# Two neighbouring tiles of the experts' tables loaded by one transfer

## The chip, the cores and the metric

The kernel runs on one core of one Trainium2 chip. The metric is the device time of one execution in microseconds; a kernel's time is the median of several runs. Besides the timed runs there is one profiled execution, which the hardware profiler recorded; all rows below are from it.

## The reference, cut to what matters

The block takes x, 512 tokens of 1024 numbers, through attention and then through a PEER layer, which holds most of the work. All is float32.

```
mix = concat(fox_attention, swa_sink_attention) @ w_out     # 512 x 1024
x   = layer_norm(ALPHA * x + mix)
# PEER: 8 heads, each picks 16 of 16384 experts per token
q   = x @ w_q ;  s1, s2 = scores of q against keys1, keys2 (128 each per head)
eidx, gate = the 16 best sums of s1 and s2, and their softmax
a   = u_tab[eidx] . x          # one number per token, head and choice
w   = gelu(a) * gate
y   = sum of w * v_tab[eidx]   # 512 x 1024
x   = layer_norm(ALPHA * x + y)
```

`u_tab` and `v_tab` have 16384 rows of 1024 floats, 64 MB each.

## The kernel before, in words

The first 350 us hold the attention and the routing (queries, scores, top 16). They load weights tile by tile as the rest does and are not touched by the change.

For 384 of the 512 tokens the kernel does not gather rows: it multiplies these tokens with the whole of both tables. Each table is 128 tiles of 128 experts x 1024 numbers, 512 KB a tile. For the 128 tokens of the first block (and for 16 of the last ones in the first table) the rows of the chosen experts are gathered by indirect transfers of 512 KB (128 rows of 4 KB) that GpSimd issues, and VectorE works on them.

The tiles are numbered through the whole kernel. In this text **feature tile n** (n = 0 to 127) is tile `S_U + n`, of the first table, and **value tile n** is tile `S_V + n`, of the second. Both `S_U` (42) and `S_V` (170) are even, and a tile's place in the ring is its number modulo 4.

What happens to every table tile c:

1. SyncE (SP) issues its load into `raw[:, c % 4, :]`, a ring of four places (`load_tile`, L436 to L439). Before it, SP waits until the tile four before it, which had the place, has been split (`lo_ready`). The load adds 16 to a semaphore of its place when it has landed.
2. ScalarE (ACT) waits for the landing and for PE to have finished tile c - 4, and rounds the tile to its upper part `hi` (`split_hi`, L451). There are four places for the parts.
3. GpSimd (POOL) writes the lower part, `lo = raw - hi` (`split_lo`, L457), and thereby frees the place in `raw`. Between two such tiles it issues the gathers (L765).
4. TensorE (PE) multiplies with both parts, in three products, so that the result has nearly float32 precision. A feature tile is 24 matmuls at lines L1831 to L1833, a value tile 18 at L1886 to L1888.

Each engine works through one list of instructions in order. What stands behind the load's consumer on ACT matters for the change:

- Feature tile n: ACT does the GELU of tile n - 4 (`gelu_tile`, L1026), then rounds tile n (L451), then, in the middle of the table, copies finished gate sums out of PSUM (`stage_gates`, L1072), then the GELU of tile n - 3. PE may begin tile n + 2 once the GELU of tile n is done, and the next group of gate matmuls (L2104, L2105) once the copy of the group before it is done.
- The last 12 feature tiles (116 to 127) keep their GELUs in SBUF (`kept`). While they are multiplied, the loads of the first value tiles are issued.
- Value tile n: ACT rounds the weights of tile n - 2 (`weight_hi`, L1118), then the table tile n (L451), then the weights of tile n - 1, and so on. VectorE (DVE) makes the weights (L1694), their lower part after ACT's part (L1703), and between them adds a gathered row (L1735). PE begins a value tile when its weights' lower part and its table parts are there.

All loads of SP go through one hardware queue (q1) and are served in the order of issue; the gathers are on another (q0), the stores of GELUs on a third (q10); all share 16 DMA engines. In the middle of the features (tiles 44 to 115) SP also stores 2 MB of gates (L602) after every sixth tile. In the values the order on SP is, per eight tiles (`load_octet`): a wait for the weights and a 768 KB load `ga`, tiles 0 to 3, a wait and the next `ga`, tiles 4 and 5, a 1.5 MB load `gg8` of gates (L649), tiles 6 and 7. Ahead of the first value tiles stand two loads of gates of 768 KB (L622), behind value tile 7 the 1 MB of layer norm parameters (L639) and one more 768 KB.

Of the kernel before, what the change touches and what calls it, by code (L numbers as in the profile page):

```python
# [27 lines left out]
P = 128  # L28
SEQ = 512
D = 1024  # L30
KT = D // P
# [9 lines left out]
ETILES = 128  # L41
# [5 lines left out]
RAW_SLOTS = 4  # L47
# [5 lines left out]
S_U = S_PQ + LISTS  # L53
S_V = S_U + ETILES
# [29 lines left out]
A_PRE = 44  # L84
# [3 lines left out]
A_MID = MID_TILES * O_MID  # L88
# [30 lines left out]
def build(nc, x_t, x_rows, w1, w_ff, b_f, sinks, ln_par, w_pq, keys_t, u_t, u_rows, v_tab, consts, out):  # L119
# [5 lines left out]
    with ctx:  # L125
        def sb(name, shape, dt=F32, stack=ctx):
            return stack.enter_context(nc.sbuf_tensor(name, shape, dt))

        def sem(name):
            return ctx.enter_context(nc.semaphore(name))  # L130
# [9 lines left out]
        raw = sb("raw", [P, RAW_SLOTS, D])  # L140
# [149 lines left out]


        raw_loaded = [sem(f"raw_loaded{i}") for i in range(RAW_SLOTS)]
        hi_ready = sem("hi_ready")
        lo_ready = sem("lo_ready")
        tile_used = sem("tile_used")
# [95 lines left out]
        def wait(eng, s, value):  # L391

            if not (isinstance(value, int) and value <= 0):
                eng.wait_ge(s, value)
# [26 lines left out]
        def parts_of(c):  # L421
            if S_WOUT + PART_SLOTS <= c < S_PQ:
                return resident[c - S_WOUT]
            if c == N_TILES - 1:
                return last_parts
            if c >= S_U:
                return hi[c % EXPERT_SLOTS], lo[c % EXPERT_SLOTS]
            return hi[c % PART_SLOTS], lo[c % PART_SLOTS]
# [7 lines left out]
        def load_tile(eng, c, it, src):  # L436

            wait(eng, lo_ready, 4 * it + (c - RAW_SLOTS + 1))
            eng.dma_start(raw[:, c % RAW_SLOTS, :], src).then_inc(raw_loaded[c % RAW_SLOTS], 16)  # L439

        def split_hi(act, c, it):

            if isinstance(it, int):
                c, it = c + 4 * it, 0
            wait(act, raw_loaded[c % RAW_SLOTS], 16 * it + 16 * (c // RAW_SLOTS + 1))
            if S_PQ <= c < S_PQ + PART_SLOTS:

                act.wait_ge(tile_used, S_WOUT + (c - S_PQ) + 1)
            elif c != N_TILES - 1 and not S_WOUT + PART_SLOTS <= c < S_PQ:
                wait(act, tile_used, 4 * it + (c - (EXPERT_SLOTS if c >= S_U else PART_SLOTS) + 1))  # L450
            act.activation(parts_of(c)[0][:, :], raw[:, c % RAW_SLOTS, :], ACT.Copy).then_inc(hi_ready, 1)  # L451
# [17 lines left out]
        KEPT = A_POST // 4  # L469
        KEPT_FROM = ETILES // 4 - KEPT  # L470
# [54 lines left out]
        def _(sp):  # L525
# [36 lines left out]
                for k in range(4):  # L562
                    load_tile(sp, S_PQ + k, i, w_pq[4 * i + k])

            for k in range(8):
                load_tile(sp, S_U + k, 0, u_t[k])

            def load_features(k, it):

                load_tile(sp, S_U + 8 + k, it, u_t[4 * it + (8 + k)])  # L570

            def move_numbers():

# [19 lines left out]
            def two_chunks(o, first=False):  # L593
                for t in range(MID_TILES):
                    load_features(t % 4, 3 * o + (A_PRE // 4 + t // 4))
                    if first and t == 3:
                        move_gates()
                    if t % (MID_TILES // 2) == MID_TILES // 2 - 1:
                        half = t // (MID_TILES // 2)

                        sp.wait_ge(staged, 4 * GROUPS_PER_CHUNK * o + 2 * GROUPS_PER_CHUNK * (half + 1))
                        sp.dma_start(g_dram[2 * o + half], stage[half][:, :, :]).then_inc(g_stored[half], 16)  # L602

            with sp.Fori(0, A_PRE // 4 - 1) as it:
                for k in range(4):
                    load_features(k, it)
            for k in range(2):
                load_features(k, A_PRE // 4 - 1)
# [9 lines left out]
            def load_group(g, slot):  # L618

                if not (isinstance(g, int) and g >= KEPT_FROM):  # L620
                    sp.dma_start(ga[slot][:, :, :], a_dram[g]).then_inc(comb_loaded[slot], 16)
                sp.dma_start(gg[slot][:, :, :, :],  # L622
                             g_dram[:, :, bass.ds(4 * g, 4), :].rearrange("c p n t -> p c n t")
                             ).then_inc(comb_loaded[slot], 16)


            for k in range(A_PRE + A_MID + 8, ETILES):
                load_tile(sp, S_U + k, 0, u_t[k])


            for slot in range(GELU_SLOTS):
# [2 lines left out]
                sp.wait_ge(g_stored[half], 16 * CHUNKS // 2)  # L634
            load_group(KEPT_FROM, 0)
            load_group(KEPT_FROM + 1, 1)
            for k in range(8):
                load_tile(sp, S_V + k, 0, v_tab[4 * KEPT_FROM + k])
            sp.dma_start(ln2_gb[:, :, :], ln_par[:, 2:4, :]).then_inc(ln_loaded, 16)  # L639
            for slot, g in enumerate((KEPT_FROM + 2, 0)):  # L640

                sp.wait_ge(wgt_ready, 4 * slot + 4)
                load_group(g, slot)
                for k in range(4):
                    load_tile(sp, S_V + 8 + 4 * slot + k, 0, v_tab[4 * g + k])

            def load_gates(i, par):

                sp.dma_start(gg8[par][:, :, :, :],  # L649
                             g_dram[:, :, bass.ds(8 * i - 4 * KEPT, 8), :].rearrange("c p n t -> p c n t")  # L650
                             ).then_inc(gg8_loaded[par], 16)
# [4 lines left out]
            def load_octet(i, par, last=False):  # L656
                for slot in range(2):
                    sp.wait_ge(wgt_ready, 8 * i + (4 * slot - 4))
                    sp.dma_start(ga[slot][:, :, :], a_dram[2 * i + (slot - KEPT)]).then_inc(comb_loaded[slot], 16)
                    for k in range(4):  # L660
                        load_tile(sp, S_V + 4 * slot + k, 2 * i, v_tab[8 * i + (4 * (slot - KEPT) + k)])
                        if slot == 1 and k == 1 and not last:
                            load_gates(i + 1, 1 - par)

            with sp.Fori(1, ETILES // 16 - 1) as j:
                for par in range(2):
                    load_octet(2 * j + par, par)
            load_octet(ETILES // 8 - 2, 0)
            load_octet(ETILES // 8 - 1, 1, last=True)
            def store_halves(b, before):  # L670
                for h in range(2):
# [142 lines left out]
        def _(act):  # L814
            for i in range(X_CHUNKS):

                act.wait_ge(xT_loaded[i], 16)
                act.activation(xT_hi[:, x_chunk(i), :], xT[:, x_chunk(i), :], ACT.Copy).then_inc(xT_hi_ready, 1)
                if i == 0:
                    split_hi(act, 0, 0)  # L820
            for c in range(1, S_LOOP):
                split_hi(act, c, 0)
# [46 lines left out]

            split_heads(1, 0, swa_k_hi, twice=swa_k_hi)  # L870
            split_hi(act, S_LOOP, 0)
            copy_proj(2, vT[:, :], 1)
            split_hi(act, S_LOOP + 1, 0)
# [1368 lines left out]
```

## Time and profile before

| | us |
|---|---|
| median of 3 runs | 1445.74 (1444.88 to 1448.5) |
| the profiled execution, its whole time | 1447.31 |
| its span in the trace | 1445.6 |
| TensorE busy (granted clock 0.998) | 1424.1 |
| GpSimd busy | 1011.6 |
| VectorE busy | 1051.2 |
| ScalarE busy | 607.4 |

The span is the time from the first to the last recorded instruction; the whole time has a little around it (1.7 us here). Busy time of TensorE leaves 21.5 us of the span. Of these 12.5 us lie in the first 350 us, where the attention starts and the phases change, and some 7 us in the last 20 us, where the last norm runs. In a row of the timeline the first number is the start, the second the duration; what stands in brackets is the idle time of the engine before the row and what ended it. In a row of the stretches stand, after the stretch and its length, the busy time (and instructions) of PE, PE's weight loads, DVE, ACT and POOL, then PE's granted clock, the share of the DMA engines and GB/s.

### The profile page before, as it was taken

Reading aid. Unit: us, or ns where it says so; the run is one execution under the profiler, and the core shown is the slowest. Engines: PE = TensorE matmul, PEld = TensorE weight load, DVE = VectorE, ACT = ScalarE, POOL = GpSimd, SP = SyncE. Lnnn points to the kernel's source line nnn. Section 1 sums busy time; section 2 is a strip of 40 time slices with the busy share of each in tenths; the row PEclk is TensorE's granted clock in tenths of the full one; section 3 lists DMA queues with packets and bytes.
Section 4 is the critical chain, followed back from the end, with each engine's and each line's share of the span. In section 5 each row is a group of like instructions: output and inputs, shape, how many; then the busy total and the mean of one; then the engine's idle time right before and its main releaser. Section 6 shows DMA issues by size and latency. Waiting matters only on the chain.

```text
span 1445.6 us, 24823 instructions
## 1 busy us (share of the span) xinstructions
PE 1424.1 (99%) x8029; PEld 1266.3 (88%) x8029; DVE 1051.2 (73%) x2206; ACT 607.4 (42%) x1018; POOL 1011.6 (70%) x629
## 2 busy tenths in 40 slices
PE   9999999999999999999999999999999999999997
PEld 5888778889999999999999999878888888888885
DVE  5466666688999999899986694867555555555587
ACT  5666741334333354444444443333333333333333
POOL 3432331335598878887887689889888888888885
PEclk9999999999999999999999999999999999999999
DMA  6212120423599979999999899999999999999981
GB/s 241 74 59 103 59 89 4 144 86 126 171 351 320 298 265 378 393 420 405 391 364 386 321 397 387 344 371 368 355 362 359 356 356 343 351 356 339 359 336 71
DMA packets 136909, 406.97 MB, mean 282 GB/s; under 512 B 13905, under 2 KB 56657, under 8 KB 134673
## 3 DMA queue, kind: packets, MB, share of 16 engines
q1 hardware_dynamic: 80384, 240.67, 46.6%
q0 software_dynamic: 39760, 142.76, 25.1%
q10 hardware_dynamic: 16704, 22.81, 4.3%
q8 instruction: 29, 0.48, 0.1%
q14 instruction: 32, 0.25, 0.0%
HBM read 355.50 MB, written 50.14 MB: 281 GB/s over the span
## 4 chain that ended last, share of the span: by engine, by line
PE 82%; DVE 5%; POOL 4%; issue 4%; DMA 2%; ACT 2%; SPq 0%; ACTq 0%; POOLq 0%; DVEq 0%
PE banks L1831 13%; PE banks L1833 13%; PE banks L1832 13%; PE banks L1886 12%; PE banks L1888 11%; PE banks L1887 11%; POOL lo L457 3%; PE banks L1948 2%; POOL rows L765 2%; PE banks L2104 1%; PE banks L2105 1%; DMA raw<-v_tab 1%; PE banks L2041 1%; PE banks L1932 1%; DVE rows L1365 1%
## 5 line engine op out<-in xcount | busy, mean ns | idle before, releaser
L457 POOL TENSOR_TENSOR lo<-raw,hi 128x1024 fp32r<-128x1024 f32 x290 | 700.5, 2417 | 344.0 <-ACT hi L451 328.0
L1831 PE MATMUL banks<-x1T_hi,hi 128*128 128x368 f32 (+3 forms) x1168 | 395.3, 338 | 0.3 <-DVE x1T_lo L1337 0.3
L1832 PE MATMUL banks<-x1T_lo,hi 128*128 128x368 f32 (+3 forms) x1168 | 390.0, 334 | 0.0
L1833 PE MATMUL banks<-x1T_hi,lo 128*128 128x368 f32 (+3 forms) x1168 | 389.9, 334 | 0.0
L451 ACT ACTIVATE hi<-raw 128x1024 fp32r<-128x1024 f32 x291 | 305.8, 1051 | 22.4 <-DMA raw<-v_tab 13.0
L1886 PE MATMUL banks<-hi,wgt_hi 128*128 128x512 f32 x750 | 292.0, 389 | 1.7 <-DVE wgt_lo L1703 1.7
L1887 PE MATMUL banks<-lo,wgt_hi 128*128 128x512 f32 x750 | 291.8, 389 | 0.0
L1888 PE MATMUL banks<-hi,wgt_lo 128*128 128x512 f32 x750 | 291.8, 389 | 0.0
L1703 DVE TENSOR_TENSOR wgt_lo<-wgt,wgt_hi 128x384 fp32r<-128x384 f32 x125 | 101.0, 809 | 185.8 <-ACT wgt_hi L1118 185.5
L1831 PEld LDWEIGHTS banks<-x1T_hi,hi 128*128 128x128 f32 x1168 | 219.3, 188 | 4.8 <-DVE x1T_lo L1337 0.6
L1833 PEld LDWEIGHTS banks<-x1T_hi,lo 128*128 128x128 f32 x1168 | 219.1, 188 | 4.4
L1832 PEld LDWEIGHTS banks<-x1T_lo,hi 128*128 128x128 f32 x1168 | 219.4, 188 | 3.9
L1118 ACT ACTIVATE wgt_hi<-wgt 128x384 fp32r<-128x384 f32 x125 | 65.6, 525 | 314.6 <-PE banks L1888 305.2
L1365 DVE CUSTOM_DVE_ANT_0 rows<-rows,banks 128x1024 f32<-128x1024 f32 x144 | 171.0, 1215 | 30.2 <-DMA rows<-u_rows,expert_at 26.5
L1026 ACT ACTIVATE gelu<-banks 128x368 f32<-128x368 f32 x116 | 55.5, 478 | 284.6 <-PE banks L1833 284.5
L1886 PEld LDWEIGHTS banks<-hi,wgt_hi 128*128 128x128 f32 x750 | 140.8, 188 | 31.6 <-DVE wgt_lo L1703 1.4
L1887 PEld LDWEIGHTS banks<-lo,wgt_hi 128*128 128x128 f32 x750 | 140.8, 188 | 29.3
L1888 PEld LDWEIGHTS banks<-hi,wgt_lo 128*128 128x128 f32 x750 | 140.8, 188 | 29.2
L1735 DVE SCALAR_TENSOR_TENSOR banks<-rows,row_weight,banks 128x1024 f32<-128x1024 f32 x128 | 164.0, 1281 | 0.7
L765 POOL DMA_INDIRECT rows<-u_rows,expert_at x144 | 140.0, 972 | 28.4 <-issue 22.2
L765 POOL DMA_INDIRECT rows<-v_tab,expert_at x128 | 127.2, 994 | 20.1 <-issue 10.3
L1694 DVE TENSOR_TENSOR wgt<-ga,gg 128x384 f32<-128x384 f32 x116 | 70.7, 609 | 0.8 <-DVE wgt_lo L1703 0.2
(240 smaller groups left out, 1753.4 us busy)
## 6 DMA issues: line engine op xcount, KB each, us to landing
raw<-u_t SPq DMA_DIRECT2D x128, 512.0 KB, 5.9
raw<-v_tab SPq DMA_DIRECT2D x128, 512.0 KB, 6.8
g_scratch<-stage SPq DMA_DIRECT2D x12, 2048.0 KB, 11.7
gelu_scratch<-gelu ACTq DMA_DIRECT2D x116, 192.0 KB
ga<-gelu_scratch SPq DMA_DIRECT2D x29, 768.0 KB, 7.7
gg<-g_scratch SPq DMA_DIRECT2D x14, 1536.0 KB, 11.5
raw<-w SPq DMA_DIRECT2D x26, 512.0 KB, 3.4
raw<-w_pq SPq DMA_DIRECT2D x16, 512.0 KB, 3.6
```

Of the source, the lines that this page charges most:

```text
L451: act.activation(parts_of(c)[0][:, :], raw[:, c % RAW_SLOTS, :], ACT.Copy).then_inc(hi_ready, 1)
L457: eng.tensor_tensor(l[:, :], raw[:, c % RAW_SLOTS, :], h[:, :].bitcast(F32), ALU.subtract).then_inc(lo_ready, 1)
L765: pool.indirect_dma_start(rows[:, k % ROWS, :], None, table, at).then_inc(gathered[k % ROWS], 16)
L1365: dve.tensor_tensor_reduce(rows[:, k, :], rows[:, k, :], x1_home, 1.0, 0.0, ALU.mult, ALU.add, dots8[:, k:k + 1]).then_inc(row_used, 1)
L1703: dve.tensor_tensor(l[:, :], wgt[k % 2][:, :], h[:, :].bitcast(F32), ALU.subtract).then_inc(wgt_lo_ready, 1)
L1735: dve.scalar_tensor_tensor(y0, rows[:, k, :], row_weight[:, bass.ds(ROWS * r + k, 1)], y0, ALU.mult, ALU.add).then_inc(row_used, 1)
L1831: pe.matmul(o, h[:, s], hiT[:, k, tokens], start=(k == 0), stop=False)
L1832: pe.matmul(o, h[:, s], loT[:, k, tokens], start=False, stop=False)
L1833: ins = pe.matmul(o, l[:, s], hiT[:, k, tokens], start=False, stop=(k == KT - 1))
L1886: pe.matmul(o, h_at(b), h[:, s], start=start, stop=False)
L1887: pe.matmul(o, h_at(b), l[:, s], start=False, stop=False)
L1888: ins = pe.matmul(o, l_at(b), h[:, s], start=False, stop=stop)
```

## The change

From tile `S_U` on two neighbouring tiles are loaded by one transfer of 1 MB (`load_pair`). SP waits until both places are free, that is for the split of tile c - 3 instead of tile c - 4, and issues one transfer into two places of the ring. It adds to a semaphore of the pair of places, and ACT waits for that semaphore before it rounds either tile. The ring keeps four places, the tiles before `S_U` stay as they are, and so does the order of all other loads between the pairs; the loads that stood between two tiles of a pair in `load_octet` (the gates, after k == 1) stand after the pair.

The first table is laid out on the host so that a partition's 8 KB of both tiles lie together in memory. The second table keeps its layout, and its pair is a transfer with 4 KB pieces (`rearrange`).

```diff
+        pair_loaded = [sem(f"pair_loaded{i}") for i in range(RAW_SLOTS // 2)]
...
+        def load_pair(eng, c, it, src):
+
+            s = c % RAW_SLOTS
+            eng.wait_ge(lo_ready, 4 * it + (c + 1 - RAW_SLOTS + 1))
+            eng.dma_start(raw[:, s:s + 2, :], src).then_inc(pair_loaded[s // 2], 16)
...
-            wait(act, raw_loaded[c % RAW_SLOTS], 16 * it + 16 * (c // RAW_SLOTS + 1))
+            if c >= S_U:
+                act.wait_ge(pair_loaded[c % RAW_SLOTS // 2], 16 * it + 16 * ((c - S_U) // RAW_SLOTS + 1))
+            else:
+                wait(act, raw_loaded[c % RAW_SLOTS], 16 * it + 16 * (c // RAW_SLOTS + 1))
...
-            for k in range(8):
-                load_tile(sp, S_U + k, 0, u_t[k])
+            for k in range(0, 8, 2):
+                load_pair(sp, S_U + k, 0, u_t[k // 2])
 
             def load_features(k, it):
 
-                load_tile(sp, S_U + 8 + k, it, u_t[4 * it + (8 + k)])
+                if k % 2 == 0:
+                    load_pair(sp, S_U + 8 + k, it, u_t[2 * it + (8 + k) // 2])
...
+            def values(tile):
+                return v_tab[bass.ds(tile, 2)].rearrange("n p d -> p n d")
...
-                    for k in range(4):
-                        load_tile(sp, S_V + 4 * slot + k, 2 * i, v_tab[8 * i + (4 * (slot - KEPT) + k)])
-                        if slot == 1 and k == 1 and not last:
+                    for k in range(0, 4, 2):
+                        load_pair(sp, S_V + 4 * slot + k, 2 * i, values(8 * i + (4 * (slot - KEPT) + k)))
+                        if slot == 1 and k == 0 and not last:
                             load_gates(i + 1, 1 - par)
...
-        "u_t": u.reshape(ETILES, P, KT, P).transpose(0, 3, 2, 1).reshape(ETILES, P, D),
+        "u_t": u.reshape(ETILES // 2, 2, P, KT, P).transpose(0, 4, 1, 3, 2).reshape(ETILES // 2, P, 2, D),
```

The loads of value tiles 0 to 15 and of the last 4 feature tiles are changed in the same way.

## Rows read from the trace of the kernel before

**Rows 1.** The page's first part: busy time, share of the span, instructions.
```profile
PE 1424.1 (99%) x8029; PEld 1266.3 (88%) x8029; DVE 1051.2 (73%) x2206; ACT 607.4 (42%) x1018; POOL 1011.6 (70%) x629
```

**Rows 2.** Busy time of each engine by stretches: middle features, change of tables, values.
```profile
550.00:650.00 100.00, 100.00 (x754) 97.83 (x754) 96.31 (x135) 47.08 (x77) 86.20 (x60) 1.00 1.01 398
...
850.00:950.00 100.00, 99.25 (x565) 91.92 (x564) 70.92 (x81) 38.39 (x55) 90.20 (x57) 1.00 0.99 371
...
1250.00:1350.00 100.00, 100.00 (x443) 82.81 (x442) 53.87 (x73) 36.33 (x50) 83.20 (x53) 1.00 0.95 353
```

**Rows 3.** The page's DMA issues: count, size, median us from issue to landing.
```profile
raw<-u_t SPq DMA_DIRECT2D x128, 512.0 KB, 5.9
raw<-v_tab SPq DMA_DIRECT2D x128, 512.0 KB, 6.8
...
rows<-u_rows,expert_at POOLq DMA_INDIRECT x144, 8.0
```

**Rows 4.** The page's group of `split_hi`: busy, mean ns, idle before and what ended it.
```profile
L451 ACT ACTIVATE hi<-raw 128x1024 fp32r<-128x1024 f32 x291 | 305.8, 1051 | 22.4 <-DMA raw<-v_tab 13.0
```

**Rows 5.** The load issued at 1226.8 us (value tile 83), its time to landing.
```profile
DMA to landing us min/median/max: 3.1/3.1/3.1
```

**Rows 6.** Chain that ended last, 945 to 985 us: start, us, what.
```profile
953.58 15.88 DMA raw<-v_tab
...
970.44 0.52 ACT wgt_hi L1118
970.98 2.45 DVE wgt_lo L1703
```

**Rows 7.** PE's timeline at 973.5 us: value tile 15 begins.
```profile
973.48 0.50 PE L1886 MATMUL banks<-hi,wgt_hi 128*128 128x512 f32 x1 [0.94 <-DVE wgt_lo L1703]
```

**Rows 8.** ACT's timeline at 972 us: value tile 17 is rounded.
```profile
971.93 1.06 ACT L451 ACTIVATE hi<-raw 128x1024 fp32r<-128x1024 f32 x1 [0.98 <-DMA raw<-v_tab]
```

**Rows 9.** SP's timeline, 886 to 903 us: issues ahead of the first value tiles.
```profile
887.35 6.13 SPq L622 DMA_DIRECT2D gg<-g_scratch  x2
893.53 9.41 SPq L439 DMA_DIRECT2D raw<-v_tab  x4
```

**Rows 10.** ACT's timeline, 895 to 925 us: value tile 0, GELU, value tile 1.
```profile
904.49 1.06 ACT L451 ACTIVATE hi<-raw 128x1024 fp32r<-128x1024 f32 x1 [3.76 <-DMA raw<-v_tab]
905.45 0.46 ACT L1026 ACTIVATE kept<-banks 128x368 f32<-128x368 f32 x1
906.68 1.06 ACT L451 ACTIVATE hi<-raw 128x1024 fp32r<-128x1024 f32 x1 [0.77 <-DMA raw<-v_tab]
```

**Rows 11.** PE's timeline at 906.1 us: the last feature tile, 127, begins.
```profile
906.12 0.33 PE L1831 MATMUL banks<-x1T_hi,hi 128*128 128x368 f32 x1
```

**Rows 12.** ACT's timeline, 924 to 945 us: value tiles 8 and 9.
```profile
934.77 1.06 ACT L451 ACTIVATE hi<-raw 128x1024 fp32r<-128x1024 f32 x1 [2.46 <-DMA raw<-v_tab]
...
936.58 1.06 ACT L451 ACTIVATE hi<-raw 128x1024 fp32r<-128x1024 f32 x1 [0.20 <-DMA raw<-v_tab]
```

**Rows 13.** PE's timeline at 939.7 us: value tile 7 begins.
```profile
939.74 0.39 PE L1886 MATMUL banks<-hi,wgt_hi 128*128 128x512 f32 x1
```

**Rows 14.** ACT's timeline, 583 to 594 us: feature tile 60, then the copy of gates.
```profile
586.91 1.05 ACT L451 ACTIVATE hi<-raw 128x1024 fp32r<-128x1024 f32 x1
...
587.86 1.02 ACT L1059 ACTIVATE banks<-x 128x1024 f32<-128x1024 f32 x1
...
588.91 1.07 ACT L1072 ACTIVATE stage<-banks 128x512 f32<-128x512 f32 x2
```

**Rows 15.** PE's timeline at 591.3 us: the next group of gate matmuls begins.
```profile
591.31 0.23 PE L2104 MATMUL banks<-gate_hi,is_i 128*128 128x128 f16 x1
```

**Rows 16.** The load issued at 578.6 us (feature tile 60), its time to landing.
```profile
DMA to landing us min/median/max: 7.8/7.8/7.8
```

**Rows 17.** The load issued at 1308.4 us (value tile 103), its time to landing.
```profile
DMA to landing us min/median/max: 7.7/7.7/7.7
```

**Rows 18.** PE's timeline at 1324.5 us: value tile 101 begins.
```profile
1324.49 0.39 PE L1886 MATMUL banks<-hi,wgt_hi 128*128 128x512 f32 x1
```

More of the change, by code:

```diff
@@ L624, in load_group @@
                              ).then_inc(comb_loaded[slot], 16)
-            for k in range(A_PRE + A_MID + 8, ETILES):
-                load_tile(sp, S_U + k, 0, u_t[k])
+            for k in range(A_PRE + A_MID + 8, ETILES, 2):
+                load_pair(sp, S_U + k, 0, u_t[k // 2])
+            def values(tile):
+                return v_tab[bass.ds(tile, 2)].rearrange("n p d -> p n d")
             for slot in range(GELU_SLOTS):
@@ L636, in _ @@
             load_group(KEPT_FROM + 1, 1)
-            for k in range(8):
-                load_tile(sp, S_V + k, 0, v_tab[4 * KEPT_FROM + k])
+            for k in range(0, 8, 2):
+                load_pair(sp, S_V + k, 0, values(4 * KEPT_FROM + k))
             sp.dma_start(ln2_gb[:, :, :], ln_par[:, 2:4, :]).then_inc(ln_loaded, 16)
@@ L643, in _ @@
                 load_group(g, slot)
-                for k in range(4):
-                    load_tile(sp, S_V + 8 + 4 * slot + k, 0, v_tab[4 * g + k])
+                for k in range(0, 4, 2):
+                    load_pair(sp, S_V + 8 + 4 * slot + k, 0, values(4 * g + k))
             def load_gates(i, par):
@@ L659, in load_octet @@
                     sp.dma_start(ga[slot][:, :, :], a_dram[2 * i + (slot - KEPT)]).then_inc(comb_loaded[slot], 16)
-                    for k in range(4):
-                        load_tile(sp, S_V + 4 * slot + k, 2 * i, v_tab[8 * i + (4 * (slot - KEPT) + k)])
-                        if slot == 1 and k == 1 and not last:
+                    for k in range(0, 4, 2):
+                        load_pair(sp, S_V + 4 * slot + k, 2 * i, values(8 * i + (4 * (slot - KEPT) + k)))
+                        if slot == 1 and k == 0 and not last:
                             load_gates(i + 1, 1 - par)
```

## The prediction, made blind

> **What bounds the kernel now.** I read the busy times first, then the same by stretches, then the waits and the chain at the few places where PE or the chain leaves the matmuls. PE is busy 1424.1 of 1445.6 us [rows 1], and in the middle of the features and in the values for the whole of a 100 us stretch [rows 2]. So PE sets the time, and no transfer can give anything back except where PE waits. Over the two tables it hardly does: 0.56 us at 527, 0.75 at 919 and 0.94 at 973 us. The last of these is the one to look at. The chain shows it [rows 6]: the load of value tile 16, issued at 953.58, landed 15.88 us later, at 969.46; ACT, which stood at its wait, then rounded the weights of tile 15 at 970.44, DVE made their lower part until 973.43, and PE began tile 15 at 973.48 after 0.94 us of idle time [rows 7]. So a late table tile does not reach PE by way of its own parts (PE would want tile 16 one tile later still) but by way of the instruction behind it on ACT. From landing to PE's start it is 973.48 - 969.46 = 4.0 us.
>
> The DMA engines are also near full: 398 GB/s at a share of 1.01 in the middle features, 371 at the change of tables, 353 in the values [rows 2]. A load of 512 KB lands in 5.9 or 6.8 us in the median [rows 3], and in 3.1 where nothing is before it in its queue [rows 5].
>
> **What the change does to a pair.** It issues the pair when the second tile was issued before, that is one tile period later for the first, and the first may be used only when both have landed. Where the queue is full all the time, the bytes up to the end of the second tile are the same as before, and the pair lands when the second tile did. Where the queue was empty, the half that went early now goes late, and the pair lands up to one step later; a step of a full queue is 936.58 - 934.77 = 1.8 us for 512 KB [rows 12]. So the first tile of each pair is late by one step (about 2 us) up to two, plus the period if it had landed early. What hides this is the lead: in steady values tile 103, issued at 1308.4, landed at 1316.1 [rows 17]. As the pair 102 and 103 it must be there 4.0 us before PE starts tile 101, at 1324.49 [rows 18], that is by 1320.5. 4.4 us of cover, against at most 1.8: nothing, in any of the octets behind value tile 24. If that cover were gone, each microsecond would cost 13, one per octet.
>
> SP issues half as many loads (0.33 us each) and has idle time between them; fewer waits on SP are worth nothing. The 128 gathers and 144 gathers are untouched. The semaphore of a pair costs nothing beside that of a tile.
>
> The cost lies where a first tile is already waited for and something that PE needs stands behind it on ACT. There are four such places.
>
> **1. Feature tiles 60 and 61, about 590 us.** ACT rounded tile 60 at 586.91, then did two further things and the copy of a gate group at 588.91 [rows 14]; PE began the next group at 591.31 [rows 15]. Tile 60 had been issued at 578.6 and landed after 7.8 us [rows 16], 0.5 us before its use. Now the pair is issued when tile 61 was, one tile period of some 4.7 us later, at 583.3. If it needed the same 7.8 us it would land at 591.1, and the copy's first half would end 1.05 + 1.02 + 0.2 + 0.54 us behind, at 593.9: 2.6 us after PE wants to begin. If the queue, which is then shorter by the early half, and the longer pieces of 8 KB bring it by 588.5, it costs nothing. I take 1.6, nearer to the upper end, since twice the bytes will hardly be quicker than the half before it; ends 0 and 3. PE, once 1.6 us later, has that much more cover at the pairs that follow, and I give those nothing.
>
> **2. Value tiles 0 and 1, 906 us.** Ahead of them stand two loads of gates whose issue held SP for 6.13 us [rows 9], so the queue is full. ACT waited 3.76 us for tile 0 until 904.49, and only then did the GELU of feature tile 125, 905.45 to 905.91; tile 1 landed at 906.68 [rows 10]. PE began feature tile 127 at 906.12 [rows 11], and it needs exactly that GELU: 0.2 us of cover. With the pair ACT is released at 906.68, 2.2 us later, and PE stalls 2.0. Nothing smaller is in sight, as the queue order is fixed; if the preceding pair (feature tiles 126 and 127) also goes later and leaves a hole in the queue, up to one step of 1.8 more. I take 2.0; ends 0 (the gates' loads land earlier, since less is ahead of them) and 3.8.
>
> **3. Value tiles 8 and 9, 940 us.** POOL's chain of splits and with it SP's issues are now 2.2 us later. Before, tile 9 landed at 936.58 [rows 12]. Value tiles 6 and 7 now go as one transfer ahead of the norm's parameters and the gates, so that the half that had gone early is in the queue before tile 8: landing 936.6 + 2.2 = 938.8, or with a step more 940.6. PE can begin tile 7 4.0 us later, at 942.8 or 944.6; it would have begun at 939.74 [rows 13] + 2.0 = 941.7. Stall 1.1 or 2.9, I take 2.0; ends 0 and 3.4.
>
> **4. Value tiles 16 and 17, 973 us.** Tile 17 landed at 971.93 [rows 8], 2.47 us after tile 16. With everything moved by the same amount, the stall of 0.94 us grows by 2.4; with a step more for the early half of tiles 14 and 15, by 4.3. I take 2.4; ends 0 and 4.4. After it the lead of the loads grows with each octet, since POOL needs 3.7 us a tile and PE 4.1.
>
> Sum: 1.6 + 2.0 + 2.0 + 2.4 = 8.0 us. On the profiled execution's own time, 1447.31, that is 1455.3; that execution stands 1.57 above the median of the runs, and on the median it is 1445.74 + 8.0 = **1453.7 us**. The four stalls add up because PE has no idle time between them in which to win one back.
>
> What the skill says for the change: the Trainium skill, DMA: Bandwidth & Descriptors, section "Anatomy of one DMA", gives each transfer a fixed 2.0 us beside bytes over 436 GB/s, hence 3.2 us for 512 KB and 4.4 for 1 MB, as an estimate of that page. By that the pair would land 1.2 us behind the single one where the queue is empty; the trace agrees for the single one (3.1). The same page asks for transfers of 1 MiB or more. Here that saves a fixed part which lies beside other transfers in the queue.
>
> **The rivals.**
>
> A: the lead hides it. The GELU of tile 125 has 0.2 us of cover only because this execution had its gates' loads land as they did; if SP's loads now reach the queue more regularly, 2 and 3 shrink to their lower ends, and 1 and 4 to half: 0.8 + 1.2 = 2.0, some 1447.7. For it: few transfers decide, and a hole in a queue is filled by gathers, which then stand less in the way later. Against: ACT's idle time for the second table is 13.0 us in all [rows 4], and 3.76 and 2.46 of it are two of the four places, so there is no lead to hide anything.
>
> B, the other side: a gain. Longer transfers keep the queue fuller, value tile 16 comes with 17 before 969.46 - 0.94, and the stall of 0.94 at 973 goes, with 0.75 at 919 at most: 1445.74 - 1.7 = 1444.0. It decides at the gates' load ahead of tile 16: it must be quicker by 3.4 us. Against it: the pair has the same bytes behind the same loads. A gain above 0.3% would need 4.3 us, and PE has not so much idle time over the tables; faster than that is all but shut out.
>
> C: the steady octets stall too. If 1 MB took twice the 7.7 us of [rows 17], the pair 102 and 103 would land at 1323.8 and PE's tile 101 start at 1327.8, 3.3 us late, 13 times: 43 us, some 1497. For it: the DMA share there is 0.95. Against: tile 103's 7.7 us are mostly the gates ahead of it.
>
> D: the gathers starve. The pieces of the first table are 8 KB now and the gathers' 4 KB; if the queues take turns by pieces, a gather beside a table load gets a third instead of a half. Gathers of the first table land in 8.0 us already [rows 3], VectorE is busy 96% of the middle features [rows 2], and POOL's split of feature tile 107 stood 7.4 us behind VectorE at 805 to 813 us, after which PE's lead was 3.0 us. Should VectorE fall back by 5 us there, PE stalls 2.0, and all the four above come on top: 1455.7. The Trainium skill, DMA: Bandwidth & Descriptors, section "Queues, rings and completion order", says that an engine goes round its queues a packet at a time; that is this rival's ground, and no row here has 8 KB table pieces to show it.
>
> That the change doesn't do what it says holds in part: the second table's pieces stay 4 KB, so for the values only the number of transfers changes. It moves no term.
>
> **How the numbers follow.** A measurement of this kernel can tell about 0.3%, 4.3 us, from no change: 1441.4 to 1450.1 is the same. The forecast, with D's small form: 0.68, of which 0.02 lies below 1450.1. A: 0.22. B: 0.05, of which 0.02 for a gain that no row explains. C: 0.05. The lower ends of the terms together give 1445.7, the upper ones 1445.74 + 3 + 3.8 + 3.4 + 4.4 = 1460.3. I leave B and C out of the range, and take A in by most: 1446.5 to 1459.5. Slower 0.66 + 0.05 = 0.71, same 0.22 + 0.03 + 0.02 = 0.27, faster 0.02.
>
> **What would show it.** In the profile after: ACT's wait for `raw<-v_tab` above 13 us in total, with the wait before value tile 0 at about 6 us instead of 3.76; an idle time of PE of about 2 us just before feature tile 127, released by ACT's GELU; one of about 2 before value tile 7 and one above 3 before value tile 15, released by the weights' lower part; one before a gate group near 591 us, released by ACT's copy; and none in the values behind 1010 us. PE's busy time and the matmuls' durations stay. It is wrong if PE's idle time between 500 and 1000 us grows by less than 3 us, or if idle time appears in every octet.

## The result, and the profile after

The changed kernel takes 1473.51 us (median of 4, 1469.2 to 1474.49) beside 1447.12 for the kernel before (1444.88 to 1449.73): 1.0183 of it, 95% interval 1.0168 to 1.0198. It is slower by 26.4 us. The forecast was slower by 8.0, with 1459.5 as its upper end. The profiled execution took 1473.96 us, its span is 1472.3 (before 1445.6).

One reading of the kernel before needs setting right: of TensorE's 21.5 us of idle time 8.5 lie in the first 350 us (busy 341.55 of 350), 2.3 between 350 and 1425.6 us and 10.8 in the last 20 (busy 9.21), not 12.5 and 7. No term of the prediction uses these.

The page first: busy time, then the groups of ACT's rounding (`split_hi`, now L461) and of the weights' lower part (now L1717), then DMA issues (count, size, median us to landing) [rows 1, 3, 4].

```profile
PE 1430.8 (97%) x8029; PEld 1268.3 (86%) x8029; DVE 1100.8 (75%) x2206; ACT 608.5 (41%) x1018; POOL 1018.1 (69%) x629
...
L461 ACT ACTIVATE hi<-raw 128x1024 fp32r<-128x1024 f32 x291 | 306.4, 1053 | 201.5 <-DMA raw<-u_t 132.9
L1717 DVE TENSOR_TENSOR wgt_lo<-wgt,wgt_hi 128x384 fp32r<-128x384 f32 x125 | 157.4, 1260 | 141.5 <-ACT wgt_hi L1132 141.0
...
raw<-u_t SPq DMA_DIRECT2D x64, 1024.0 KB, 8.0
raw<-v_tab SPq DMA_DIRECT2D x64, 1024.0 KB, 7.7
gg<-g_scratch SPq DMA_DIRECT2D x14, 1536.0 KB, 14.6
```

A landing takes 8.0 us instead of 5.9 for twice the bytes. That doesn't mean that the queue carries more, since two or more single loads were under way at once before; the stretches below show that it carries less. ACT waits 201.5 us before it rounds, where it waited 22.4. PE is busy 6.7 us longer for the same 8029 instructions, and the remaining 20 us of the difference are idle time of PE. The stretches [rows 2]: after start and length come the busy times of PE, its loads, DVE, ACT and POOL, then the granted clock, the DMA share and GB/s.

```profile
550.00:650.00 100.00, 91.28 (x673) 88.53 (x671) 91.79 (x132) 41.15 (x68) 81.43 (x58) 0.98 0.97 378
850.00:950.00 100.00, 95.07 (x581) 90.03 (x579) 66.20 (x80) 37.88 (x57) 87.57 (x56) 1.00 0.94 362
1250.00:1350.00 100.00, 98.93 (x435) 81.23 (x434) 79.99 (x73) 36.16 (x49) 84.64 (x52) 1.00 0.91 345
```

In the middle features PE lost 9 of 100 us, and every engine does less; the DMA engines too, at 378 GB/s instead of 398, though with a share of 0.97 they are nearly full in both. No engine's share rose there, so this loss is time in which the engines wait for each other. What PE waited for, by line (us in total, times, longest):

```profile
PE banks L2118 <- ACT stage L1086: 9.9, 5, 3.5
PE banks L1900 <- DVE wgt_lo L1717: 8.6, 7, 3.0
PE banks L1845 <- ACT kept L1040: 2.9, 1, 2.9
```

The first is new: the gate matmuls wait for ACT's copy of the last group. The second was 1.7 us in 2 waits before. PE's timeline has each of them with its place: four gate groups in the middle features, then feature tile 127, value tiles 7 and 15, and much later value tile 101.

```profile
556.19 0.22 PE L2118 MATMUL banks<-gate_hi,is_i 128*128 128x128 f16 x1 [1.61 <-ACT stage L1086]
...
597.93 0.23 PE L2118 MATMUL banks<-gate_hi,is_i 128*128 128x128 f16 x1 [2.50 <-ACT stage L1086]
...
629.71 0.23 PE L2118 MATMUL banks<-gate_hi,is_i 128*128 128x128 f16 x1 [3.46 <-ACT stage L1086]
...
922.71 0.43 PE L1845 MATMUL banks<-x1T_hi,hi 128*128 128x368 f32 x1 [2.93 <-ACT kept L1040]
...
957.34 0.47 PE L1900 MATMUL banks<-hi,wgt_hi 128*128 128x512 f32 x1 [0.70 <-DVE wgt_lo L1717]
...
993.23 0.80 PE L1900 MATMUL banks<-hi,wgt_hi 128*128 128x512 f32 x1 [2.97 <-DVE wgt_lo L1717]
...
1347.16 0.50 PE L1900 MATMUL banks<-hi,wgt_hi 128*128 128x512 f32 x1 [1.07 <-DVE wgt_lo L1717]
```

Why 3.46 us at 629.71: ACT's timeline just before it. The rounding of feature tile 66, whose pair landed at 628.1, stands ahead of the copy (L1086) that PE needs. This is the mechanism of the prediction, an instruction behind the late tile on ACT, at 630 us and at two other groups besides the one that it had named (near 591 us, here at 597.93).

```profile
628.11 1.06 ACT L461 ACTIVATE hi<-raw 128x1024 fp32r<-128x1024 f32 x1 [4.93 <-DMA raw<-u_t]
628.12 0.34 ACTq L1048 DMA_DIRECT2D gelu_scratch<-gelu  x1
629.08 1.06 ACT L1086 ACTIVATE stage<-banks 128x512 f32<-128x512 f32 x2
```

**Where the 26.7 us went.** I took the starts of tiles' first matmuls in both traces and subtracted the lengths of the stretches between them; for the kernel before they are 140.5 us (feature tiles 44 to 74), 153.5 (to 107), 86.7 (to 127), 54.0 (to value tile 12), 50.2 (to 24) and 435.3 to the end. The table has what each kernel's profiled execution took more, with the experiments below (e8 changes the kernel before; its span is 2.1 us shorter than that one's). Each row is a single execution. How far two executions of the same instructions differ shows where rows share their code: e5 and e10 load and use the features as the changed kernel does and have 11.0 and 8.0 in F44–F74, beside 11.4; e9 has 5.7 in F127–V12, beside 1.1. Differences of 3 to 5 us in one column are no effect of an edit by themselves.

| more than before, us | span | start to F44 | F44–F74 | F74–F107 | F107–F127 | F127–V12 | V12–V24 | V24–end |
|---|---|---|---|---|---|---|---|---|
| changed kernel | 26.7 | 0.8 | 11.4 | 0 | 4.4 | 1.1 | 3.4 | 5.6 |
| e1 late issue | 7.7 | 0.1 | 4.0 | 0 | 3.1 | 0.3 | 0.3 | 0 |
| e2 joint wait | 6.7 | 0.2 | 3.9 | 0 | 2.3 | 0.2 | 0.3 | 0 |
| e3 both | 44.2 | 1.2 | 12.8 | 8.9 | 6.3 | 2.0 | 4.8 | 8.2 |
| e4 pieces 4 KB | 37.8 | 2.0 | 13.8 | 5.3 | 5.0 | 4.5 | 0.1 | 7.0 |
| e5 features only | 11.7 | -0.1 | 11.0 | 0 | 1.9 | 0.2 | -1.2 | 0 |
| e6 values only | 6.6 | -0.1 | 0 | 0 | 1.2 | 1.8 | 3.7 | 0 |
| e7 gates first | 21.6 | 0.7 | 6.2 | 0.4 | 3.8 | 3.3 | 0.2 | 7.0 |
| e9 numbers first | 21.8 | 0.1 | 9.3 | 0 | 4.5 | 5.7 | -0.7 | 2.9 |
| e10 ring of eight | 15.2 | 1.0 | 8.0 | 0 | 4.8 | 1.1 | 0.3 | 0 |
| e11 e7 and e9 | 12.3 | 0.1 | 2.8 | 0.9 | 3.5 | 2.9 | 2.1 | 0 |
| e12 all three | 10.7 | 1.5 | 2.3 | 1.2 | 3.8 | 1.6 | 0.3 | 0 |

**The clock.** Part of PE's longer busy time is a lower granted clock. Two short stretches right behind the two longest idle times, and for comparison the one behind the idle time of 2.93 us:

```profile
631.00:634.40 3.40, 3.40 (x13) 3.40 (x12) 3.40 (x6) 1.43 (x3) 3.23 (x3) 0.50 1.05 426
993.00:996.40 3.40, 3.17 (x8) 2.55 (x9) 3.40 (x4) 1.48 (x2) 3.38 (x2) 0.53 0.52 150
922.70:926.00 3.30, 3.29 (x20) 3.29 (x21) 0.00 (x0) 2.33 (x3) 3.12 (x3) 1.00 0.21 84
```

Behind 3.46 and 2.97 us of idle time the clock was at 0.5 (1.2 instead of 2.4 GHz) for 3.41 us each, at most 1.7 us lost each; behind 2.93 us it stayed at 1.00. So each of those two stalls costs up to half as much again. The length of the idle time alone doesn't decide it: in e9's trace the clock also fell at idle times of 2.54 and 2.43 us (before 595.03 and 627.10 us), in e1's it did not behind 2.44 (before 623.13 us).

### The profile page after: what moved, and what is told of

Read it like the earlier page. It is cut to its first block, busy times and chain, and to the rows that moved or that the text cites. A ratio compares the mean times of both kernels' runs of the same rounds, so it can differ in the third digit from the quotient of the medians.

```text
span 1472.3 us, 24386 instructions
## 1 busy us (share of the span) xinstructions
PE 1430.8 (97%) x8029; PEld 1268.3 (86%) x8029; DVE 1100.8 (75%) x2206; ACT 608.5 (41%) x1018; POOL 1018.1 (69%) x629
## 4 chain that ended last, share of the span: by engine, by line
PE 62%; DVE 11%; POOL 10%; issue 8%; DMA 6%; ACT 2%; SPq 1%; ACTq 0%; POOLq 0%; DVEq 0%
PE banks L1845 9%; PE banks L1847 9%; PE banks L1900 9%; PE banks L1846 9%; PE banks L1902 9%; PE banks L1901 9%; POOL lo L467 6%; POOL rows L779 4%; DMA raw<-u_t 2%; PE banks L1962 2%; DVE rows L1379 2%; DMA raw<-v_tab 2%; DMA rows<-u_rows,expert_at 1%; DVE gate_hi L1609 1%; DVE gate_lo L1610 1%
## 5 line engine op out<-in xcount | busy, mean ns | idle before, releaser
L461 ACT ACTIVATE hi<-raw 128x1024 fp32r<-128x1024 f32 x291 | 306.4, 1053 | 201.5 <-DMA raw<-u_t 132.9
L1717 DVE TENSOR_TENSOR wgt_lo<-wgt,wgt_hi 128x384 fp32r<-128x384 f32 x125 | 157.4, 1260 | 141.5 <-ACT wgt_hi L1132 141.0
L779 POOL DMA_INDIRECT rows<-v_tab,expert_at x128 | 134.1, 1048 | 20.4 <-issue 13.2
```

What stands on the lines that cost most here:

```text
L779: pool.indirect_dma_start(rows[:, k % ROWS, :], None, table, at).then_inc(gathered[k % ROWS], 16)
L1717: dve.tensor_tensor(l[:, :], wgt[k % 2][:, :], h[:, :].bitcast(F32), ALU.subtract).then_inc(wgt_lo_ready, 1)
```

## The experiments

All times are medians beside the kernel before on the same chip (1445.64, 1445.85 and 1445.33 us for e1 to e4, e5 to e8, e9 to e12).

### One part of the pair alone: late issue, joint wait, both

e1 keeps the transfers of 512 KB; SP waits before the first of two for both places:

```diff
-            wait(eng, lo_ready, 4 * it + (c - RAW_SLOTS + 1))
+            last = c + 1 - c % 2 if c >= S_U else c
+            wait(eng, lo_ready, 4 * it + (last - RAW_SLOTS + 1))
```

> The kernel before, with single transfers of 512 KB and a semaphore each; only SP waits, before the first tile of a pair, until both places are free, and then issues both. Theory H (the ring hands over in pairs: both loads start when the second could, and the first tile may be used only when both are there; a late tile reaches PE through what stands behind it on ACT): this is one half of the change, so it costs a part of the 26 us, 5 to 15 us, 1452 to 1462, with PE waiting for ACT's gate copies near 600 us. Rival S (it is the size and the 8 KB pieces of the transfers that hold the queue and the other transfers up): nothing of the change is in this kernel but half of the waits, 1447 to 1450.

e2 issues as before, but ACT waits for both landings:

```diff
+            if c >= S_U and c % 2 == 0:
+                act.wait_ge(raw_loaded[(c + 1) % RAW_SLOTS], 16 * it + 16 * ((c + 1) // RAW_SLOTS + 1))
```

> The kernel before, with single transfers issued as before; only ACT, before it rounds the first tile of a pair, waits for the second tile's landing too. Theory H: the other half, and by my own prediction the whole of the stall before feature tile 127 (2 us) and the growth of the one before value tile 15 (2.4 us): 1450 to 1458. Rival S: 1447 to 1449.

e3 has both edits.

> Both of these together: the handing over in pairs of the changed kernel, with transfers of 512 KB. Theory H: the loss is all here, 1467 to 1478, with the clock's two drops and the drift behind 1150 us. Rival S: below 1455.

Measured: e1 1453.28 (1.0050, interval 1.0033 to 1.0067), e2 1455.53 (1.0074, 1.0057 to 1.0091), e3 1491.66 (1.0313, 1.0295 to 1.0330). Each half is cheap, +7.6 and +9.9, as expected, and the two together cost +46.0: 28.5 more than their sum, 20 more than the changed kernel, and 14 above the expectation for e3, which had wanted all of the changed kernel's loss there and no more. So the loss doesn't come from one of the halves but from both at once, and the 1 MB transfers are no cause of it: at the same rule for issuing and using, they give some 20 us back. Waits of PE in e3, to be read beside those of the changed kernel above:

```profile
PE banks L2107 <- ACT stage L1075: 12.4, 11, 2.5
PE banks L1889 <- DVE wgt_lo L1706: 9.8, 8, 3.0
```

What makes it more than a sum is the lead, the time from a tile's landing to the start of its rounding on ACT (start of the rounding in ACT's timeline, less the landing of its load):

| lead, us | F48 | F50 | F52 | F54 | F56 | F58 | F60 |
|---|---|---|---|---|---|---|---|
| before | 9.2 | 9.3 | 8.2 | 4.9 | 2.9 | 0.0 | 0.5 |
| e1 late issue | 6.6 | 4.1 | 1.6 | 0.0 | 0.0 | 0.0 | 0.0 |
| changed kernel | 0.6 | 0.0 | 0.0 | 0.0 | 0.0 | 0.0 | 0.0 |

The late issue takes 2.6, 5.2 and 6.6 us of it at tiles 48, 50 and 52; a joint wait takes the time between two landings. Before, the lead was 8 to 9 us up to tile 52 and ran out only at 58, and the kernel just got through. Late issue alone runs out at 54.

The two halves feed each other: a late landing makes a late split, and a late split a late issue. Feature tile 44 was issued at 501.2 us before, at 505.2 in e1, at 501.3 in e2, but at 508.1 in e3 and 510.3 in the changed kernel. Its lead of 9.1 us before is 0.0 there, more than the two amounts of a single pair would take. From tile 48 to tile 72 the changed kernel issued a tile every 5.07 us, where it was 4.68 before (523.55 to 645.2 against 517.6 to 629.9), which was PE's own 140.5 / 30. That the ring is then slower than PE, and not held back by PE, is argued from this and not shown by it.

A lead of 0 is not yet a loss. In the changed kernel it is 0.0 at every pair from F16 to F46 too, and the way to F44 costs 0.8 us: POOL's split of these tiles still ended 1.9 us or more before PE began them. What lies behind F44 and not before it are the gate groups, whose copies stand behind the rounding on ACT. From F78 to F106 the leads are 0.6 to 3.9 us in the changed kernel and nothing is lost; in e3 they are 0.1, and F74–F107 costs 8.9. That is half of the 17.5 us between the two traces.

### The layout

e4 is the changed kernel with the first table in its old layout, so that all pieces are 4 KB:

```diff
-                load_pair(sp, S_U + k, 0, u_t[k // 2])
+                load_pair(sp, S_U + k, 0, u_t[k:k + 2].rearrange("n p d -> p n d"))
...
-        "u_t": u.reshape(ETILES // 2, 2, P, KT, P).transpose(0, 4, 1, 3, 2).reshape(ETILES // 2, P, 2, D),
+        "u_t": u.reshape(ETILES, P, KT, P).transpose(0, 3, 2, 1).reshape(ETILES, P, D),
```

> The changed kernel, but the first table in its old layout, so that its 1 MB transfers have 4 KB pieces like the second table's. Theory H: no matter, within 3 us of the changed kernel's 1473.5. Rival S in the form in which the 8 KB pieces take the gathers' turns: 10 us or more come back, and gathers of the first table land in 8 us instead of later.

Measured: 1479.2 (1473.77 to 1485.1), 1.0218 (1.0180 to 1.0256). Theory H missed its 3 us and the rival its 10: the intervals of the ratio overlap with the changed kernel's, so the time may be the same or longer, but nothing like 10 us comes back. The issues in e4, beside 8.0 us for the features' pairs and 9.7 for the gathers of `u_rows` in the changed kernel (8.0 before [rows 3]):

```profile
raw<-u_t SPq DMA_DIRECT2D x64, 1024.0 KB, 9.3
...
rows<-u_rows,expert_at POOLq DMA_INDIRECT x144, 11.5
```

In this execution both the pairs and the gathers land later with 4 KB pieces. It was the slowest of e4's runs, which fall into two groups (1474.0 and 1473.8, 1484.4 and 1485.1), so how much of it is the layout stays open. Gathers of the first table do land later in the changed kernel, as rival D had it, but not for the reason it gave: with 4 KB pieces everywhere they take 9.3 us in e1 and 10.9 in e3. The stall that D feared behind feature tile 107 did not come either; F74–F107 costs nothing in the changed kernel.

### One table alone

e5 pairs the features and loads the values as before, e6 the other way round (in each `load_pair` goes back to `load_tile` for the other table, and ACT's wait with it; in e6 the first table's layout too).

```diff
-            for k in range(0, 8, 2):
-                load_pair(sp, S_U + k, 0, u_t[k // 2])
+            for k in range(8):
+                load_tile(sp, S_U + k, 0, u_t[k])
```

> Pairs in the first table only, the second table by single transfers. Theory H, from the trace after: the idle times of PE before gate groups (1.6, 1.1, 2.5, 3.5 and 1.2 us) stay, with one drop of the clock, and so does part of the 2.9 before feature tile 127; the rest (0.8, 0.7, 3.0, four of about 1.1 behind 1340, the second drop) goes: 1458 to 1463.

> Pairs in the second table only. Theory H: the idle times before gate groups are gone, 2 to 3 us before feature tile 127, 2 to 3 before value tile 15 with a drop of the clock, and the drift behind 1150 us with its four idle times stay: 1456 to 1462. If the drift is a consequence of what the features left behind, it goes too: below 1455.

Measured: e5 1460.51 (1455.59 to 1462.93), 1.0094 (1.0066 to 1.0122); e6 1458.75 (1453.88 to 1464.7), 1.0087 (1.0060 to 1.0114). +14.7 and +12.9 make 27.6, the changed kernel's 26.4. Within the spread of these runs the tables are additive, and each costs more than the whole forecast. e6's runs spread over 11 us; its profiled execution was one of the two shortest (1453.94), and there no octet behind value tile 24 lost anything. So the late stalls of the values are not in every execution of it.

### The instruction behind the late tile

e7 is the changed kernel with the copy of a gate group ahead of the rounding on ACT, e8 the same edit on the kernel before:

```diff
+                if between is not None:
+                    between()
...
-                        gelu_tile(tile % 4, 3 * o + (A_PRE // 4 + tile // 4))
+                        gelu_tile(tile % 4, 3 * o + (A_PRE // 4 + tile // 4), between=gates)
```

> The changed kernel, but on ACT the copy of a gate group stands ahead of the rounding of the table tile instead of behind it. Theory H with ACT's order as the way to PE: PE's 9.9 us of waiting for the gate copies fall below 2, and the clock's first drop goes with them: 1460 to 1466. If the late tiles reach PE by their own parts, the waits turn into waits for the split and the time stays at 1470 to 1476.

> The kernel before with the same order on ACT as in e7. It has no waits of PE for the copies, so by theory H nothing changes: 1446 to 1449. If rounding 1.6 us later costs lead, more.

Measured: e7 1469.62 (1462.96 to 1472.08), 1.0151 (1.0119 to 1.0184); e8 1446.3, 1.0002 (0.9992 to 1.0012). e8 shows that the order itself costs and gives nothing. e7's trace shows the waits for `stage` gone and others in their place:

```profile
PE banks L1903 <- DVE wgt_lo L1720: 7.1, 5, 2.6
PE banks L1848 <- POOL lo L467: 4.2, 3, 3.3
PE banks L1848 <- ACT kept L1040: 3.3, 1, 3.3
```

F44–F74 costs 6.2 us instead of the 8.0 to 11.4 of the four executions with these pairs and the old order (the changed kernel, e5, e9 and e10), and PE now meets the late tiles by way of POOL's split as well. The expectation, 1460 to 1466, was too good: in the median only some 2.6 us come back (+23.8 beside +26.4), inside the spread. That the order on ACT is a way to PE is shown by the waits; that taking it away alone makes the kernel faster is not.

### Who is late first: the numbers of the experts

In the changed kernel SP issues the eight small transfers of the expert numbers (`move_numbers`) behind the pair 48/49, since that pair is issued as a whole. POOL waits for them before its gathers; its timeline after, then before:

```profile
533.36 0.19 POOL L772 COPY expert_at<-small 128x8 uint32<-128x8 uint32 x1 [4.83 <-DMA small<-row_weight]
```

```profile
527.77 0.19 POOL L758 COPY expert_at<-small 128x8 uint32<-128x8 uint32 x1 [2.85 <-DMA small<-row_weight]
```

POOL is 5.6 us later there, and so is its split of tile 48. e9 issues the numbers first:

```diff
-            for k in range(2):
-                load_features(k, A_PRE // 4 - 1)
             move_numbers()
-            for k in range(2, 4):
+            for k in range(4):
                 load_features(k, A_PRE // 4 - 1)
```

> The changed kernel, but SP issues the eight small transfers of expert numbers (ready at 518 us) ahead of the pair of feature tiles 48 and 49 instead of behind it. Theory N (in the changed kernel these stand behind the pair on SP and behind its 1 MB in the queue, so that GpSimd waits 4.8 us for them and its chain of splits goes on 5.6 us later than before, in the stretch where GpSimd has no idle time to catch up; that is why the pairs up to feature tile 74 lose 11.4 us and not 1.6): that stretch loses 5 us or less, 1464 to 1469. Rival (the stretch loses its time because each pair's 1 MB lands late beside the gathers, whatever came before it): it stays within 2 us of 11.4, 1471 to 1476.

e11 has e9's and e7's edit.

> The changed kernel with both: numbers ahead of the pair, gate copies ahead of the rounding. If the stretch from feature tile 44 to 74 loses its time by these two ways alone, it loses less than 2 us now; the change of tables and the values as in the changed kernel: 1456 to 1464.

Measured: e9 1468.93 (1465.75 to 1472.65), 1.0162 (1.0138 to 1.0185); e11 1460.47 (1459.49 to 1462.17), 1.0106 (1.0089 to 1.0123). In e9 POOL's copy starts at 528.56 and the leads of F48 to F52 come back in part (1.7, 3.8, 0.4 us), but they are again 0 from F54 on, and the stretch still costs 9.3 us. My theory had wanted 5 or less: it missed. Since 9.3 lies between the 8.0 of e10 and the 11.4 of the changed kernel, which have neither edit, the trace doesn't show that the numbers by themselves cost anything in this stretch. Together with the copy moved ahead, F44–F74 falls to 2.8 us (2.3 in e12), well below all of them though not below the expected 2, and the kernel to +15.1, 11.3 us less than the changed kernel, with intervals of the ratio that don't touch. Part of that is no work of the edits: the traces put 5.6 us of it into the octets behind value tile 24, which neither edit changes. So the two help together in F44–F74, and neither clearly alone.

### The depth of the ring

e10 gives the second table eight places from value tile 16 on, so four pairs instead of two; nothing else of the order is changed:

```diff
+            n = (c - S_V) % 8
+            if not second:
+                eng.wait_ge(lo_ready, 4 * it + (c + 1 - 8 + 1))
...
+            eng.dma_start(at, src).then_inc(eight_loaded[n // 2], 16)
```

> The changed kernel, but from value tile 16 on the ring has eight places, so that four pairs are in it instead of two. Theory H: the features lose what they lose in the changed kernel, but behind value tile 24 PE never waits (4.6 us between value tiles 54 and 120 in the trace after, 1 us behind), and no pair is waited for by ACT there: 1464 to 1470. Rival (the drift comes from the transfers' load on the queue itself): the drift stays, 1471 to 1476.

e12 has e7, e9 and e10.

> The changed kernel with numbers first, gates first and the ring of eight from value tile 16. What is left is the change of tables (feature tile 107 to value tile 24), some 9 us after by its trace: 1452 to 1459. Not below the kernel before, since PE has nothing to win.

Measured: e10 1469.24 (1462.45 to 1473.86), 1.0173 (1.0153 to 1.0194); e12 1459.23 (1458.0 to 1466.17), 1.0110 (1.0083 to 1.0136). ACT's waits for the second table, in the changed kernel and then in e10:

```profile
ACT hi L461 <- DMA raw<-v_tab: 63.7, 32, 6.6
```

```profile
ACT hi L486 <- DMA raw<-v_tab: 16.3, 5, 6.4
```

With eight places ACT waits 5 times, all between 918 and 985 us, and V24 to the end costs 0 instead of 5.6 us. From value tile 24 to 122 the lead of a pair is 2.8 us or more, where it is 0 at 26 of 50 pairs in the changed kernel. So more places give more lead. That the four places are the reason for the stalls is not shown, for the executions of e6 and e11 have four and lose nothing there either; e11's ACT waits 8 times for the second table, 22.8 us in all. In the time e10 gives 2.5 us (+23.9 beside +26.4), inside the spread of both, and its profiled execution was its shortest; e12 beside e11 gives 1.2.

None of these comes below the kernel before. e12, 0.2 us above its expected range and the best of those that pair both tables, keeps 2.3 us in F44–F74 and 5.4 between F107 and V12, where PE waits 3.2 us for ACT's GELU before feature tile 127 as it does in the changed kernel.

## Why the prediction was right in direction and wrong in size

**Right.** The way of the loss: a late tile reaches PE by the instruction behind it on ACT. Place 2: 2.93 us before feature tile 127, released by ACT's GELU, for 2.0 forecast (ends 0 and 3.8). ACT's wait for value tile 0 was 6.04 us for "about 6". Places 3 and 4: 1.1 + 3.4 = 4.5 us in the stretches F127–V24 for 4.4, which is luck: up to 1.7 of it is the clock, and the stalls alone were over-priced, above all value tile 7 with 0.70 us of idle time for "about 2". Place 1 itself, the group that the prediction named, waited 2.50 us for 1.6 (ends 0 and 3). ACT's waits for the second table grew from 13.0 to 63.7 us. A and B (hidden, or a gain) are refuted, and C in its size (43 us).

**Wrong, place 1: 1.6 forecast, 11.4 measured.** The step that failed is "PE, once 1.6 us later, has that much more cover at the pairs that follow, and I give those nothing". The working looked only at tiles 60 and 61, where the lead was nearly gone, and asked by how much they come later. It did not ask which other tiles have a lead below what the pair takes away, one tile period of 4.7 us and the 1.8 us of a step. By the table of leads above that is every pair from tile 54 on, and even this is too little: F44 to F52 had leads of 7.6 to 9.3 us and kept 0.0 to 0.6, since the delays of the pairs before add up. The stalls came at four gate groups (1.61, 1.14, 2.50 and 3.46 us, 8.7 together), and 1.7 of clock on top makes 10.4 of the 11.4. Nor did PE's delay give cover: the loads are issued by POOL's progress, and this is delayed by the landings as well.

**Wrong, the steady octets: 0 forecast, 5.6 measured** (not in each experiment's execution). The step was "4.4 us of cover, against at most 1.8". The pair 102/103 took this long to land, where tile 103 took 7.7 [rows 17]:

```profile
DMA to landing us min/median/max: 11.9/11.9/11.9
```

It was issued at 1331.26, 14.8 us before PE could have begun tile 101 (1346.09), where tile 103 was issued 16.1 us before that [rows 17, 18]: 1.3 lost by the issue and 4.2 by the landing are 5.5, against 4.4 of cover, and the stall is 1.07. The 1.5 MB of gates ahead of the pair landed 15.0 us after their issue instead of 11.5: they stand behind a whole pair, issued 0.6 us before them. That this lengthens the pair's landing follows from the order in the queue; no run here takes it away. It is the "step more for the early half" which the prediction allowed at places 3 and 4 and left out here. C had the right mechanism and was priced by doubling a landing, not by the queue. Of the 13 octets only the last four stalled; the lead wears off slowly before that, and PE is busy for the whole of 1020 to 1330 us. Why it wears off in this execution and not in those of e6 and e11 is open.

**A term that was missing.** Small things ahead of a queue: the expert numbers behind a pair (5.6 us on POOL; what they cost PE isn't shown), a gate group at 855.84 (1.21 us, in F107–F127), the clock behind two stalls (up to 3.4 us of PE's 6.7 us of extra busy time). "PE's busy time stays" was wrong.

**The sum.** 11.4 + 4.4 + 1.1 + 3.4 + 5.6 + 0.8 = 26.7, against 1.6 + 2.0 + 2.0 + 2.4 + 0 = 8.0. Of the 18.7 us that were missed, 9.8 are place 1 and 5.6 the octets.

Open: why e9 and e7 win so little alone and so much together; which part of the spread of some 10 us between runs of e4, e6, e7 and e10 is whether a stall grows long enough for the clock to fall (e3's profiled execution has five such falls, e9's four, e1's none over the two tables); whether a ring of eight for the features too, which was not tried, would hide the whole.

## What to carry to other kernels

In a ring of few places, a transfer of two units costs lead twice: one period because it is issued when the second place is free, and the gap between two landings because neither is usable before both are. Before pairing, list for every unit the lead (landing to first use) and compare it with period plus step; where it is below that, don't look for a single stall but for a loop of landing, use and issue, whose period may exceed that of the engine which sets the time. The comparison is a lower bound (F44 lost 9.1 us of lead, not 6.5), and a lead of 0 costs nothing while the parts behind it are still ahead of that engine and nothing else stands behind the late unit. Neither half of the cost may be judged alone: 7.6 and 9.9 us here, 46 together. And compare one trace with one trace only after looking at two of the same code: here they differ by 3 us and more in a stretch.

## What was not expected of the hardware

- **DVE's lower part beside POOL's split.** `wgt_lo` takes 0.56 us alone and 2.44 when it begins beside POOL's split, as here ahead of value tile 101 in the changed kernel:

```profile
1344.31 2.39 POOL L467 TENSOR_TENSOR lo<-raw,hi 128x1024 fp32r<-128x1024 f32 x1 [4.23 <-ACT hi L461]
```

```profile
1344.67 2.44 DVE L1717 TENSOR_TENSOR wgt_lo<-wgt,wgt_hi 128x384 fp32r<-128x384 f32 x1 [3.76 <-ACT wgt_hi L1132]
```

A late tile releases both at once, so 1.9 of the 4.0 us from landing to PE's start are this meeting; over the kernel `wgt_lo` went from 101.0 to 157.4 us. The Trainium skill, SBUF — State Buffer, section "SBUF: two separate sides", says that an operation of VectorE with two inputs in SBUF and one of GpSimd that reads SBUF exclude each other for the whole instruction; the trace agrees, as `wgt_lo` ends 0.4 us behind the split.
- **1 MB against 512 KB.** With nothing ahead in its queue a pair landed after 4.7 to 4.8 us (feature tiles 0 to 5), the single tiles 0, 2 and 4 before after 3.1 to 3.2 (3.1 in [rows 5] too): 1.5 to 1.7 us for the second half. By the two-part fit of the Trainium skill, DMA: Bandwidth & Descriptors, section "Anatomy of one DMA", which is given for transfers that GpSimd issues, it would be 1.2, an estimate.
- **The clock** fell for 3.41 us (6.83 in some) at single idle times of 2.4 to 4.1 us, in the middle of a stretch that is otherwise busy, and at others of 2.44 to 2.93 us it stayed.
